# Expert weights in twelve places instead of ten: four whole experts held ahead, gate and up issued by SyncE, down by ScalarE

## The reference, cut to what matters

```python
def _hier_moe(h, w_group, b_group, w_expert, b_expert, w_gate, w_up, w_down):
    ...  # softmax over 4 groups, best group, then the best 2 of its 8 experts, with weights
    expert_id = g_sel[:, None] * MOE_EXPERTS_PER_GROUP + top_idx
    ...
    def expert_block(args):
        xb, e = args
        return (jax.nn.silu(xb @ w_gate[e]) * (xb @ w_up[e])) @ w_down[e]
```

## Time and profile before

| | |
|---|---|
| time, median of 3 runs | 2392.76 us (2388.86 to 2394.88) |
| profiled execution: its time, its span | 2387.12 us, 2385.3 us |
| PE busy in the span | 2071.5 us (87%) |
| DVE, ACT busy | 1169.6 us (49%), 824.5 us (35%) |
| bytes moved by DMA | 662.59 MB, mean 278 GB/s |
| passes of the expert loop (runs of L1604) | 70 in both layers |

### The profile page before, as it was taken

How to read it: one execution, slowest core, us unless ns; L and a number is a source line. 1 busy time by engine, 2 the same in 40 slices (tenths; PEclk the granted TensorE clock), 3 DMA queues, 4 the chain that set the end, 5 groups by cost and what they waited for, 6 DMA issues and landing times.

```text
span 2385.3 us, 47175 instructions
## 1 busy us (share of the span) xinstructions
PE 2071.5 (87%) x17804; PEld 1569.8 (66%) x17805; DVE 1169.6 (49%) x2331; ACT 824.5 (35%) x1618; POOL 25.9 (1%) x40
## 2 busy tenths in 40 slices
PE   7999878666779987666687999989999999998997
PEld 3567545444448955343354888877887888877886
DVE  4677412111116632111113776766666766766666
ACT  2232211111115411111112654545555554555554
POOL 0000000000000000000000000100001000100001
PEclk9999999888989999888898999999999999999999
DMA  9874999999995589999998746343555546343552
GB/s 393 334 283 180 428 430 431 431 431 431 431 421 222 208 339 431 431 431 431 432 431 316 246 145 209 107 142 108 195 152 178 195 144 215 107 139 110 194 152 78
DMA packets 273332, 662.59 MB, mean 278 GB/s; under 512 B 6064, under 2 KB 200624, under 8 KB 248112
## 3 DMA queue, kind: packets, MB, share of 16 engines
q1 hardware_dynamic: 264416, 532.99, 58.9%
q10 hardware_dynamic: 8784, 127.86, 12.5%
HBM read 659.78 MB, written 1.05 MB: 277 GB/s over the span
## 4 chain that ended last, share of the span: by engine, by line
PE 73%; DMA 13%; DVE 5%; another core or an unknown queue 4%; issue 3%; ACT 1%; SPq 1%; DVEq 0%; ACTq 0%; PEldq 0%
PE ps L2183 20%; PE ps L2188 10%; PE ps L1575 10%; DMA arena<-in_moe_w_up 6%; PE ps L2457 4%; PE ps L1604 4%; DMA A<-in_moe_w_up 4%; PE ps L1557 2%; DMA ring<-in_moe_w_up 2%; PE ps L2622 2%; PE ps L1523 2%; PE ps L1986 1%; PE ps L1988 1%; PE ps L1987 1%
## 5 line engine op out<-in xcount | busy, mean ns | idle before, releaser
L2183 PE MATMUL ps<-XS,WS 128*128 128x512 f32 x1408 | 499.4, 400 | 9.2 <-DVE XS L685 8.1
L2168 DVE TENSOR_TENSOR WS<-ring,WS 128x1024 fp32r<-128x1024 f32 (+1 forms) x276 | 329.3, 1194 | 226.6 <-ACT WS L2163 226.3
L2163 ACT CAST WS<-ring 128x1024 fp32r<-128x1024 f32 (+1 forms) x276 | 283.0, 1026 | 330.2 <-PE ps L2188 312.3
L2188 PE MATMUL ps<-XS,WS 128*128 128x256 f32 x1408 | 393.9, 280 | 0.0
L1861 DVE TENSOR_TENSOR arena<-arena,ps 64x256 f32<-64x256 f32 x70 | 29.6, 423 | 624.3 <-ACT arena L1669 624.3
L2183 PEld LDWEIGHTS ps<-XS,WS 128*128 128x128 f32 x1408 | 265.5, 189 | 81.4 <-DVE XS L685 18.3
L2188 PEld LDWEIGHTS ps<-XS,WS 128*128 128x128 f32 x1408 | 266.5, 189 | 0.2 <-issue 0.2
L1575 PE MATMUL ps<-arena 128*32 128x256 f32 x1632 | 166.6, 469 | 102.2 <-DMA arena<-in_moe_w_up 50.8
L1575 PE MATMUL ps<-ring,arena 128*32 128x256 f32 x2240 | 163.1, 455 | 101.0 <-DMA ring<-in_moe_w_up 88.0
L2183 PE MATMUL ps<-HS,WS 128*128 128x512 f32 x616 | 217.0, 398 | 0.0
L1575 PEld LDWEIGHTS ps<-arena 128*32 128x32 f32 x1632 | 94.3, 134 | 169.8 <-issue 149.7
(11 more groups left out here) (354 smaller groups left out, 3104.3 us busy)
## 6 DMA issues: line engine op xcount, KB each, us to landing
ring<-in_moe_w_down ACTq DMA_DIRECT2D x60, 2048.0 KB, 13.7
ring<-in_ffn_w_gu SPq DMA_DIRECT2D x90, 1024.0 KB, 7.4
ring<-in_moe_w_gate SPq DMA_DIRECT2D x32, 2048.0 KB, 43.4
ring<-in_moe_w_up SPq DMA_DIRECT2D x32, 2048.0 KB, 48.8
arena<-in_moe_w_gate SPq DMA_DIRECT2D x32, 2048.0 KB, 43.3
ring<-in_w_mod SPq DMA_DIRECT2D x24, 2048.0 KB, 12.0
ring<-in_ffn_w_down SPq DMA_DIRECT2D x32, 1408.0 KB, 6.4
arena<-in_moe_w_up SPq DMA_DIRECT2D x16, 2048.0 KB, 49.4
```

The source lines that it names most:

```text
L2163: L.inc(L.eng.copy(self.parts(u)[0], source), self.w_high)
L2168: L.inc(L.eng.tensor_tensor(wl, self.unit(u)[1], high(wh), ALU.subtract), self.w_split)
L2183: L.eng.matmul(ps[:, bank, :].rearrange("p (j t) -> p j t", j=2), wh[:, i, :], moving[:, :, k, :], start=k == 0, stop=False)
L2188: mm = L.eng.matmul(ps[:, bank, 0:TL], wl[:, i, :], moving[:, 0, k, :], start=False, stop=k == total - 1)
```

## The change

There are twelve places of one matrix in a Moe stage. `EXTRA` goes from 3 to 4 (places 6 to 9 in the arena, A is place 10), and a new tensor `SPARE` is place 11; its memory comes from a smaller DMA scratch area (`SCRATCH = 256` bytes, so that the first tensor starts at byte 512 rather than 16640). All three matrices of an expert are now four experts ahead: SP issues the 12 matrices of experts 0 to 3 before the loop, in an order of places given by hand, then gate and up of e + 4 as before, and ACT issues down of e + 4 rather than e + 2. For the last four experts ACT issues nothing.

To keep the arena places free earlier, the small tensors that live during the expert loop are moved below `EXTRA_AT` or into RS, the router's scratch is placed inside place 6, and the attention's long-lived tensors are moved to the start of the arena. In layer 0 places 7, 8 and 9 wait for the end of attention (`mla.outs_copied`), not for `norms[1]`; SPARE waits for nothing. Place 6, the last of the twelve (down of expert 3), waits until the router's table is kept (`table_kept`, L1854).

Behind the loop SP waits for experts 28, 29 and 30 in turn and issues the loads of the next stage whose places that expert frees.

```diff
-EXTRA = 3
-AHEAD, DOWN_AHEAD = 4, 2
+EXTRA = 4
+AHEAD = 4
 A_PLACE = RING + EXTRA
+SPARE_PLACE = A_PLACE + 1
+RING_2_ORDER = (1, 3, 2, 0)
+SCRATCH = 256
...
-FIRST_BYTE = 16640
+FIRST_BYTE = SCRATCH + 256
...
+        SPARE = sb("SPARE", [P, SLOT])
...
-                near = [(self.first + i) % RING for i in range(RING)]
-                far = [RING + i for i in range(EXTRA)] + [A_PLACE]
-                places = {"moe_w_gate": (near[0], near[3], far[0], far[2]), "moe_w_up": (near[1], near[4], far[1], far[3]),
-                          "moe_w_down": (near[2], near[5])}
+                assert len(order) == len(set(order)) == 3 * AHEAD
                 for e in range(EXPERTS):
...
-                    for name in ("moe_w_gate", "moe_w_up", "moe_w_down"):
-                        plan(self.rows_of(w[name][l][e]), (1, SLOT), done, places[name][e % len(places[name])])
+                    for j, name in enumerate(("moe_w_gate", "moe_w_up", "moe_w_down")):
+                        plan(self.rows_of(w[name][l][e]), (1, SLOT), done, order[3 * (e % AHEAD) + j])
...
-                per_turn = 16 * (AHEAD // DOWN_AHEAD if which == 2 else 1)
-                eng.wait_ge(slot_in[place_of[n]].sem, turn * per_turn + arrivals[n])
+                eng.wait_ge(slot_in[place_of[n]].sem, turn * 16 + arrivals[n])
...
-                    src = w["moe_w_down"][self.l][bass.ds(turn * AHEAD + (a + DOWN_AHEAD), 1)].rearrange("o (p c) n -> p o (c n)", p=P)
+                    src = w["moe_w_down"][self.l][bass.ds(turn * AHEAD + (a + AHEAD), 1)].rearrange("o (p c) n -> p o (c n)", p=P)
...
                 for a in range(AHEAD):
-                    blocks = expert(EXPERTS // AHEAD - 1, a)
-                    if a < AHEAD - DOWN_AHEAD:
-                        load_down(EXPERTS // AHEAD - 1, a, blocks)
+                    expert(EXPERTS // AHEAD - 1, a)
...
-                self.slots = [plan(piece, (KD, 512), (self.w_split, 4 * i + 4)) for i, piece in enumerate(pieces)]
+                self.slots = [plan(piece, (KD, 512), (self.w_split, 4 * i + 4), at)
+                              for i, (piece, at) in enumerate(zip(pieces, (SPARE_PLACE, 0, 1, 3, 5, 2, 4, 0)))]
...
-        moes[0] = Moe(0, TL, norms[1])
+        late = [RING + i for i in range(1, EXTRA)]
+        moes[0] = Moe(0, TL, norms[1], (SPARE_PLACE, *late, 0, 1, 3, 5, 2, 4, A_PLACE, RING))
         conv = Conv()
-        moes[1] = Moe(1, TL, norms[3])
+        moes[1] = Moe(1, TL, norms[3], (SPARE_PLACE, 1, 3, 5, 2, 4, 0, *late, A_PLACE, RING))
...
-                moe = next((m for m in moes if m.first == n - RING), None)
+                moe = next((m for m in moes if m.first == n), None)
...
-                sp.wait_ge(stages_done.sem, 3 * (1 + first_stack.index(moe.norm)))
-                for e, j in ((2, 0), (2, 1), (3, 0)):
-                    load(moe.first + 3 * e + j)
-
-                sp.wait_ge(moe.rows_turned.sem, moe.rows_turned.base + moe.NT)
-                load(moe.first + 3 * 3 + 1)
-
-
-                sp.wait_ge(moe.ranges.sem, moe.ranges.base + 1)
+                for n in range(moe.first, moe.first + 3 * AHEAD):
+                    if place_of[n] == late[0]:
+                        if moe is moes[0]:
+                            sp.wait_ge(mla.outs_copied.sem, mla.outs_copied.base + mla.UNITS_Q)
+                        else:
+                            sp.wait_ge(stages_done.sem, 3 * (1 + first_stack.index(moe.norm)))
+                    if place_of[n] == A_PLACE:
+                        sp.wait_ge(moe.rows_turned.sem, moe.rows_turned.base + moe.NT)
+                    if place_of[n] == RING:
+                        sp.wait_ge(moe.table_kept.sem, moe.table_kept.base + 1)
+                    load(n)
...
-                sp.wait_ge(moe.down.sem, blocks_through(EXPERTS - 2))
-                sp.sem_inc(spare.sem, 1)
                 n = moe.first + 3 * EXPERTS
+                last_blocks = [(e, blocks_through(e)) for e in range(EXPERTS - AHEAD, EXPERTS - 1)]
+                for e, blocks in last_blocks:
+                    sp.wait_ge(moe.down.sem, blocks)
+                    sp.sem_inc(spare.sem, 1)
+                    while (before[n] - moe.first) // 3 == e:
+                        load(n)
+                        n += 1
...
-    nc = bacc.Bacc("TRN2", target_bir_lowering=False, num_devices=1)
+    nc = bacc.Bacc("TRN2", target_bir_lowering=False, num_devices=1, dynamic_dma_scratch_size=SCRATCH)
```

More of the change, by code:

```diff
@@ L240, in vcol, with carver @@
             return VECS[:, VEC[name] + shift:VEC[name] + shift + width]
-        def carver():
-            used = [0]
+        def carver(first=0):
+            used = [first]
             def take(width):
@@ L258, in program @@
         stages_done = sig("stages_done")
-        slot_in = [sig(f"slot_in{i}") for i in range(A_PLACE + 1)]
+        slot_in = [sig(f"slot_in{i}") for i in range(SPARE_PLACE + 1)]
         spare = sig("spare")
@@ L273, in slot @@
                 return A[:, :, :].rearrange("p k n -> p (k n)")
+            if at == SPARE_PLACE:
+                return SPARE[:, :]
             return arena[:, EXTRA_AT + (at - RING) * SLOT:EXTRA_AT + (at - RING + 1) * SLOT]
@@ L278, in plan @@
             if at is None:
-                at = (n - second_stack[0]) % RING_2 if second_stack else n % RING
+                at = RING_2_ORDER[(n - second_stack[0]) % RING_2]
             before.append(max((i for i in range(n) if place_of[i] == at), default=None))
@@ L887, in program @@
         take = carver()
[L888 to L896, removed]
         ACC = [take(TA) for _ in range(3)]
@@ L902, in program @@
         SMALL = take(16)
-        PL = [arena[:, 8 * TA + 4 * D + i * 2 * TA:8 * TA + 4 * D + (i + 1) * 2 * TA].rearrange("p (j n) -> p j n", j=2) for i in range(2)]
+        PTL = [take(4 * P).rearrange("p (k t) -> p k t", k=4) for _ in range(2)]
+        CQ = take(4 * TL).rearrange("p (c t) -> p c t", c=4)
+        KT = take(HEADS * TA).rearrange("p (h t) -> p h t", h=HEADS)
+        V = take(4 * D).rearrange("p (t c) -> p t c", t=4)
+        latents_at = take.used()
+        CKV = take(2 * TA).rearrange("p (c t) -> p c t", c=2)
+        after_latents = take(2 * TA)
+        assert latents_at - HEADS * TA - 4 * D <= EXTRA_AT + SLOT
+        KPE = take(TA)
+        QRAW, T1, QR = (take(TL) for _ in range(3))
+        QN = take(2 * TL).rearrange("p (j t) -> p j t", j=2)
+        PL = [arena[:, latents_at + i * 2 * TA:latents_at + (i + 1) * 2 * TA].rearrange("p (j n) -> p j n", j=2) for i in range(2)]
         SQ = [after_latents[:, 0:TA], after_latents[:, TA:2 * TA]]
@@ L1366, in program, with __init__ @@
         class Moe:
-            def __init__(self, l, tokens, norm):
+            def __init__(self, l, tokens, norm, order):
                 self.l, self.T, self.NT, self.norm = l, tokens, tokens // P, norm
@@ L3000, in load_expert @@
                     e = turn * AHEAD + a
-                    sp.wait_ge(moe.hidden.sem, blocks_through(e))
+                    blocks = blocks_through(e)
+                    sp.wait_ge(moe.hidden.sem, blocks)
                     for j, name in enumerate(("moe_w_gate", "moe_w_up")):
```

30 lines of the change are left out of this document (16 added, 14 removed).

## The result

The kernel with twelve places takes 2359.19 us (median of 4 runs, 2358.83 to 2370.77), the kernel before on the same chip 2391.35 us (4 runs, 2388.86 to 2394.88). The ratio is 0.9884, 95% interval 0.9866 to 0.9902. (Two numbers are compared here: the medians of several executions, and the two executions that were profiled.)

The account below looks back on a forecast made before the run. The prediction took the expert stages to be bound by DMA at 431 GB/s, 4.87 us a matrix. Layer 0's -9.8 and layer 1's -9.9 make -19.7 us, from 2392.8 to 2373.1 us, range 2366 to 2382.

Parts of the forecast that it names:

- The count of matrices: Expert stages: from the first reissue, matrices left times 4.87 us plus about 4 us give the start expert 31's weights allow.
- PE in the tail, layer 0: -9.8 forecast: Layer 0's last experts: expert 31 starts 8.1 us earlier, and its hidden products take 1.7 us less.
- Rival (a): Last experts: PE at the low clock sets the tail, 12.4 us from start to start; -11.0 us, 2381.8; chance 0.11.
- Layer 1: -9.9 forecast: Layer 1's last experts: expert 31 starts 8.4 us earlier, and its hidden products take 1.5 us less.
- The next stage's loads: Conv and feed-forward pieces issued when experts 28, 29 and 30 end: neither gain nor cost, priced at nought.
- rival (b): End of expert stages: the next stage's loads overtake gate and up of expert 31; +9.5 us, 2402; chance 0.06.
- Moved scratch: Tensors change place in SBUF, no instruction is added or waits more: priced at nought.
- The sum: Whole kernel: -9.8 and -9.9 us from the two layers make -19.7 us.
- rival (d): More than the sum: arrivals decide everywhere, -22.1 us, 2370.7, or conv or feed-forward gains at full clock; chance 0.09.
- The base and the range: Whole kernel: -19.7 us taken from the timed median of 2392.8 gives 2373.1; range 2366 to 2382.
- Rival (c): Expert stages: DMA-limited, so a deeper store changes nothing; 0 to 3 us in both layers, 2390 to 2393; chance 0.06.

Follow-up runs that it names:

- ten_places: Kernel after with down again two experts ahead and only ten matrices loaded ahead of the loop; 2386.67 us, ratio 0.9997 to the kernel before.
- late_start: Kernel after, but SP issues none of layer 0's twelve matrices until its norm may begin; 2382.93 us in one run.
- late_twelfth: Kernel after, but the twelfth matrix waits for expert 0's hidden products and goes out at the first reissue; 2372.06 us in one run.
- b_again: The kernel before, unchanged, profiled a second time; 2386.36 us, ratio 0.9999 to the kernel before.
- layout_only: Kernel before with only the tensors outside the arena moved to where the kernel after has them, ten places kept; 2388.71 us, ratio 1.0003.
- a_again: The kernel after, unchanged, profiled a second time; 2364.78 us, ratio 0.9905 to the kernel before.
- a_third: The kernel after, unchanged, repeated on another chip; 2369.03 us, ratio 0.9922 to the kernel before.
- redraw: Kernel after with one more 128x512 matmul, result unused, in front of weight unit 20 of each feed-forward; 2367.26 us in one run.
- held_next: Kernel after with the next stage's loads held until expert 30 is finished, as before the change; 2366.65 us in one run.
- b_one_queue: Kernel before (down two ahead), with SP issuing all the loop's transfers, down included, in one queue; 2393.82 us in one run.
- one_queue: Kernel after, but SP issues down too, behind gate and up of the same expert, and ACT none; 2362.24 us, ratio 0.9895 to the kernel before.

## Why the prediction was right and wrong

**The count of matrices: right.** In layer 0 the first reissue stood at 273.0, and 84 x 4.87 + 4 puts the start that expert 31's weights allow at 686.0; PE started it at 687.4, 1.4 us later. Up of 29 landed at 666.4, 80 matrices after the reissue by the same count (666.6). The rate inside the full stretch did not change. ten_places, late_start and late_twelfth move 2, 3.7 and 1 matrices across the boundary and are 9.9, 19.0 and 4.9 us longer in layer 0: 4.9 to 5.1 us for each, against 4.87.

**PE in the tail, layer 0: -9.8 forecast.** From the norm's load to the next it is 10.9 in the two profiles shown and 10.8 between the means of the table (before, b_again, layout_only and ten_places against after, a_again, a_third, redraw and held_next). The term that was mis-sized: 12.4 us from expert 29 to 30, made of the slow pass 11.3 and a change of expert 1.1. It took 11.1 (666.83 to 677.95), since its hidden products took 5.07 us and not 6.28. Rival (a), 12.4 us twice, did not come.

**Layer 1: -9.9 forecast, -7.6 in the two profiles shown, -8.7 between the means.** What failed here is "expert 29 starts at 1250.3 without a wait, so 30 at 1260.6 and 31 at 1270.3". I took PE's start of expert 29 over from the trace before as if nothing ahead of it moved. But it hangs on expert 27, whose weights now come after the rest of the twelfth matrix (4.87 less the 3.5 us that it was early, 1.4) and whose first hidden products took 6.36 us where before they took 5.35, in the chain before:

```profile
1220.32 5.35 PE ps L1575 x64
```

Expert 27 starts 366.1 us behind the reissue, not 364.2, and expert 29 397.2 us, not 394.2. (In late_start, where expert 27's took 5.35 us again, expert 31 started 49.3 us behind it and not 50.3.) From expert 27's first pass on nothing waits for weights any more, and PE, not transfers, sets the end: 844.3 + 1.4 + 84 x 4.87 + 4 is 1258.8, PE starts expert 31 at 1260.65.

**A term that was missing: the norm behind the experts.** PE's sums of squares follow the last pass. The timeline of PE at the end of layer 1, before and then after:

```profile
1291.82 5.41 PE L730 MATMUL ps<-A,BASE 128*128 128x256 f32 x16 [1.01 <-ACT A L709]
```

```profile
1272.24 3.72 PE L736 MATMUL ps<-A,BASE 128*128 128x256 f32 x16 [1.01 <-ACT A L715]
```

TensorE no longer waited ahead of the last pass, so the sixteen products behind it run at the full clock too. The stretches that hold them, before and then after (columns as in the table by stretch):

```profile
1291.82:1297.20 5.38, 5.38 (x16) 4.09 (x16) 2.23 (x6) 4.17 (x9) 0.00 (x0) 0.68 0.91 308
```

```profile
1272.24:1275.90 3.66, 3.66 (x16) 2.91 (x16) 2.24 (x6) 3.55 (x8) 0.00 (x0) 1.00 1.09 386
```

The granted clock is 0.68 before and 1.00, that is 2.4 GHz, after. The last norm is 19.1 us in the four kernels that wait there and 17.8 in those that don't, b_one_queue among them; one_queue, which waits again, has 5.40 and 19.2. In layer 0 the sums got shorter in the same way (5.41 to 3.72), and the next stage's first product came 1.1 us behind the table load and not 2.8; but the conv stage as a whole did not get shorter (116.9 to 117.4). Its second ten us, before and then after:

```profile
724.20:734.20 10.00, 8.21 (x48) 7.30 (x49) 7.24 (x17) 9.31 (x19) 0.00 (x0) 0.83 0.33 129
```

```profile
711.78:721.78 10.00, 9.39 (x44) 8.28 (x45) 7.96 (x17) 7.95 (x16) 0.00 (x0) 0.66 0.85 331
```

The granted clock is 0.66 there and not 0.83, and in the first twenty us of the stage PE did 64 matmuls where it did 72 before: the head start is given back. Ahead of it, in the first ten us, PE was busy for 7.3 us after and for 8.9 before. Conv and the norm behind it take 122.3 to 122.6 us in 13 of the 14 profiles, whichever way the stage began.

**The next stage's loads: right.** held_next shows nought, and rival (b) is out with it.

**Moved scratch: right.** layout_only (tensors outside the arena) and ten_places (those inside it too) show nought.

**The sum.** By stages, between the means: 10.8 + 8.7 + 1.4 = 20.9 us; forecast 19.7. The medians of 2386.9 (25 runs on the chip of b_again) and 2365.7 (14 runs in three sets) give 21.2; set by set, each against the kernel before on its own chip, it is 32.2, 22.1 and 18.9. The mechanism was right. That its size came out right to 1.2 us is in part luck: layer 0 gave 1.0 more than forecast, layer 1 1.2 less, and the norm's 1.4 was not in the sum. It lies near rival (d)'s 22.1, but (d) is not what happened: PE's pace, not arrivals, set the last experts' starts.

**The base and the range: wrong, and this is the step that failed.** "2392.8 - 19.7 = 2373.1" and the range from 2366 take every stage but the two expert stages as fixed, and put what changes there at nothing without a reason. The runs showed that the feed-forwards alone move an execution by up to four times 3 us, with no line of them changed: their sum is 704.0 us in the profile after, 712.9 in a_again and 710.2 in a_third, three executions of one kernel. So -6.5 us of the -27.8 between the first two profiles was their pace. The base itself was a median of three runs that lies 5.9 us above that of 25; the profiled execution would have been the better one: 2387.1 - 19.7 = 2367.4, inside the range but still 8.2 us above what was measured. The kernel after ran at 2359 in three of its first four runs, and at 2365 and 2369 (medians) in the next two sets. Why that first set was so fast is seen only for the profiled execution, where all four feed-forwards had the fast pace; for the others it is argued. Were each feed-forward drawn by itself, all four would be under 178 us in one execution of nine (30 of 52 were), so three executions of four would be rare luck; whether the draws of one set hang together stays open.

**Small slips of the recorded working.** 274.4 + 84 x 4.87 + 4 is 687.5 and not 687.6. Slice 15 (339 GB/s) is not at the full rate, and slice 12 (421) nearly is. Neither changes a term.

**Rival (c), no change, and the page beside it.** The rule of the Trainium skill (DMA: Bandwidth & Descriptors, Issuing engines are not separate DMA queues), that another issuing engine brings no bandwidth, holds in all full stretches (431 GB/s). It did not decide, since the gain was idle time ahead of them. Order is a matter of its own: one_queue and b_one_queue have the bytes and the rate of their bases and differ from them by -9 and +10 us in the sum of both layers.

## What to carry to other kernels

In a stage that is bound by transfers, count them: from the first reissue on, its length is the number of transfers left times their price, and here a place in memory was worth one of them only where DMA had idle time to fill it, and in full only until PE set the end (two places gave 9.3 us up to expert 31 in layer 0 and 6.2 in layer 1). A second queue let its loads overtake; in this kernel that made a shallow buffer for them enough and cost one transfer at the end, so choose it by depth. Before forecasting to 0.5%, find out from repeated runs which stages that the change doesn't touch change by themselves, and put that into the range.

## What the runs showed of the hardware

The long streams of float32 matmuls in the feed-forwards have two paces at one granted clock. The 128x512 matmuls of one line in the second feed-forward, before and then after:

```profile
L2183 PE MATMUL ps<-XS,WS 128*128 128x512 f32 x333 | 117.7, 399 | 0.0
```

```profile
L2189 PE MATMUL ps<-XS,WS 128*128 128x512 f32 x333 | 115.5, 391 | 0.0
```

And the stretch as a whole, before and after:

```profile
1649.70:1829.00 179.30, 179.30 (x1035) 1.00 0.57 182
```

```profile
1628.20:1804.25 176.05, 176.05 (x1035) 1.00 0.57 185
```

The same 1035 matmuls, PE busy all the time, the granted clock 1.00 in both, and 3.25 us between them, 1.8%; the 128x512 matmul takes 399 ns against 391. It was the slow pace in 22 of 52 feed-forwards (13 profiles, redraw left out). In all 52 it is kept from the start of the stream to its end, and redraw shows it changed by one instruction, four times of four; what makes the pace stays open.
